# Who makes the remainders of the first mixer's output-projection weights: two chunks from VectorE to GpSimd

## The reference

```python
def hgrn2_mixer(h, w_in, lower_bound, g_norm_w, w_out):
    q, f, i, g = jnp.split(h @ w_in, 4, axis=-1)
    ...
    fg = lb + (1.0 - lb) * jax.nn.sigmoid(heads(f))
    o = hgrn2_chunkwise(jax.nn.silu(heads(q)), 1.0 - fg, heads(i), jnp.log(fg))
    o = o * lax.rsqrt(jnp.mean(jnp.square(o), -1, keepdims=True) + RMS_EPS)
    o = o * g_norm_w.astype(jnp.float32) * jax.nn.silu(heads(g))
    return o.reshape(B, S, D).astype(h.dtype) @ w_out
```

## Time and profile before

| | |
|---|---|
| median of three runs | 1483.66 us (1483.12 to 1487.24) |
| span of the profiled execution | 1483.1 us |
| busy: PE, DVE, ACT, POOL | 1452.5, 859.6, 615.7, 482.5 us |
| the last mixer iteration | about 225 to 255 us |

### The profile page before, as it was taken

The page is one execution under the profiler, slowest core; times in us unless marked ns, Lnnn a source line. Parts: engine busy times, 40 slices in busy tenths (PEclk is TensorE's granted clock), DMA queues, the critical chain, the costliest instruction groups (busy, mean ns, idle before and its releaser), DMA issues.

```text
span 1483.1 us, 23698 instructions
## 1 busy us (share of the span) xinstructions
PE 1452.5 (98%) x9390; PEld 1207.6 (81%) x9390; DVE 859.6 (58%) x1261; ACT 615.7 (42%) x780; POOL 482.5 (33%) x360
## 2 busy tenths in 40 slices
PE   8999999999999999999999999999999999999999
PEld 6787887898888888899777988888888897777677
DVE  7787686576665660165686666656630374565741
ACT  5565554353223221245574442232221355655541
POOL 0000000225544545432221145445454524422222
PEclk9999999999999999999999999999999999999999
DMA  7422122403222233323102122222323312322211
GB/s 222 136 74 87 58 86 102 156 29 114 85 92 106 87 112 113 112 87 106 66 30 86 57 86 85 95 103 88 110 85 112 129 58 86 130 74 71 72 56 59
DMA packets 23601, 137.25 MB, mean 93 GB/s; under 512 B 2600, under 2 KB 5208, under 8 KB 8672
## 3 DMA queue, kind: packets, MB, share of 16 engines
q1 hardware_dynamic: 18288, 124.79, 23.9%
q10 hardware_dynamic: 5232, 11.32, 2.8%
HBM read 131.89 MB, written 4.21 MB: 92 GB/s over the span
## 4 chain that ended last, share of the span: by engine, by line
issue 41%; PE 27%; POOL 24%; DVE 3%; DMA 2%; ACT 1%; DVEq 1%; POOLq 0%; ACTq 0%; SPq 0%
POOL WL L468 15%; POOL WL L477 9%; PE pair L503 7%; PE pair L505 6%; PE pair L504 6%; DMA RAW<-stream 1%; PE pair L1096 1%; PE pair L1083 1%; DVE WL L1672 1%; PE pair L688 1%; PE pair L1015 1%; PE pair L1073 1%; PE pair L717 1%; ACT WH L1202 1%; DMA PAR<-params 0%
## 5 line engine op out<-in xcount | busy, mean ns | idle before, releaser
L503 PE MATMUL pair<-AH,WH 128*128 128x512 f32 (+1 forms) x1240 | 473.4, 382 | 9.4 <-DVE AL L1661 6.6
L468 POOL TENSOR_TENSOR WL<-RAW,WH 128x512 fp32r<-128x512 f32 x228 | 310.5, 1394 | 475.6 <-ACT WH L1202 475.6
L505 PE MATMUL pair<-AH,WL 128*128 128x512 f32 (+1 forms) x1240 | 462.6, 373 | 0.0
L504 PE MATMUL pair<-AL,WH 128*128 128x512 f32 (+1 forms) x1240 | 462.4, 373 | 0.0
L1202 ACT ACTIVATE WH<-RAW 128x2048 fp32r<-128x2048 f32 x106 | 202.8, 1913 | 455.5 <-PE pair L505 446.4
L477 POOL TENSOR_TENSOR WL<-RAW,WH 128x512 fp32r<-128x512 f32 x128 | 171.8, 1374 | 506.8 <-ACT WH L1202 506.8
L503 PEld LDWEIGHTS pair<-AH,WH 128*128 128x128 f32 x1240 | 233.5, 188 | 58.5 <-issue 15.9
L505 PEld LDWEIGHTS pair<-AH,WL 128*128 128x128 f32 x1240 | 233.0, 188 | 41.8
L504 PEld LDWEIGHTS pair<-AL,WH 128*128 128x128 f32 x1240 | 233.5, 188 | 41.1 <-issue 1.9
L2042 DVE TENSOR_SCALAR CA<-pair,PAR 128x512 f32<-128x512 f32 x88 | 67.3, 806 | 147.4 <-PE pair L505 144.4
L503 PE MATMUL pair<-GH,WH 128*128 (+2 forms) x416 | 148.7, 357 | 0.1
(11 more groups left out here) (249 smaller groups left out, 1890.4 us busy)
## 6 DMA issues: line engine op xcount, KB each, us to landing
RAW<-stream SPq DMA_DIRECT2D x114, 1024.0 KB, 4.9
H<-x_t SPq DMA_DIRECT2D x5, 512.0 KB, 6.6
bias_rows<-ROWS ACTq DMA_DIRECT2D x1, 2048.0 KB, 24.5
BIAS<-bias_rows ACTq DMA_DIRECT2D x1, 2048.0 KB, 7.8
FBC<-forget_rows ACTq DMA_DIRECT2D x4, 512.0 KB, 4.0
out<-H ACTq DMA_DIRECT2D x8, 256.0 KB, 2.0
H<-x_t SPq DMA_DIRECT2D x1, 1024.0 KB, 10.4
RAW<-stream SPq DMA_DIRECT2D x3, 256.0 KB, 6.7
```

The lines of the kernel that those rows point to most:

```text
L468: pool.tensor_tensor(WL[w][:, part], RAW[raw][:, part], WH[w][:, part].bitcast(F32), ALU.subtract).then_inc(w_lo, 1)
L503: pe.matmul(out_, wh, xh, start=start, stop=False, skip_group_check=shared)
L504: pe.matmul(out_, wh, xl, start=False, stop=False, skip_group_check=shared)
L505: return pe.matmul(out_, wl, xh, start=False, stop=stop, skip_group_check=shared)
```

## The change

Chunks 16 and 17 leave `BY_DVE`: VectorE's two calls of `split_lo` in the last iteration go, and with them the row form in `split_lo`. GpSimd's first span starts two chunks earlier and covers four chunks. The counts follow: SP's loads of chunks 18 and 19 and TensorE's first uses of chunks 16 and 17 wait on `w_lo`, no longer on `hg_lo`.

```diff
-        BY_DVE = range(1, N_HO + 2)
+        BY_DVE = range(1, N_HO)
...
-            return 4 * (n + (-1 - N_HO - (extras_before(n) if skip is None else skip)))
+            return 4 * (n + (1 - N_HO - (extras_before(n) if skip is None else skip)))
...
-            span(split_rows, N_HO + 2, 2)
+            span(split_rows, N_HO, 4)
...
-                    if part % 2 == 0 or n >= N_HO:
+                    if part % 2 == 0:
...
-                    if n >= N_HO:
-                        raw, wh, wl = (a.rearrange("p (k c) -> p k c", k=2) for a in (raw, wh, wl))
...
-                        part = (slice(None), slice(None), slice(512 * half, 512 * half + 512)) if n >= N_HO else (slice(None), slice(1024 * half, 1024 * half + 1024))
+                        part = (slice(None), slice(1024 * half, 1024 * half + 1024))
...
-                split_lo(HG_F[it + 1] if not last else N_HO)
+                if not last:
+                    split_lo(HG_F[it + 1])
...
-                split_lo(HG_V[it + 1] if not last else N_HO + 1)
+                if not last:
+                    split_lo(HG_V[it + 1])
```

## The result

The changed kernel takes 1488.67 us (median of 15 runs, 1487.15 to 1490.13), the kernel before 1484.34 us in the same comparison (15 runs, 1483.06 to 1488.96). The recorded ratio is 1.0024 with an interval of 1.0017 to 1.0031 (the two medians by themselves are 4.3 us apart, a quotient of 1.0029). So the change costs 2.5 to 4.6 us, most likely 3.6. That is real, since the interval leaves out 1; it lies under the prediction's bound of 0.3% by the ratio, while the upper end of the interval lies just above it.

What follows compares the result with a forecast made beforehand. VectorE's chain into TensorE's hole ahead of level 5 was taken to bound the change. Terms 0 + 0 + 3.3 = +3.3 us on the median 1483.66 gave 1486.96, rounded 1487.0; range 1484.0 to 1488.8.

Steps and rivals of the forecast that it cites:

- rival (b): Ahead of level 5: all four GpSimd quarters precede line 1733, since ScalarE is not held up; +4.1 us, 1487.8, chance 0.18.
- the forecast of two or three quarters ahead: Second set, chunk 17: two or three GpSimd quarters precede line 1733; 1485.9 or 1487.0 us, chance 0.55.
- rival (c): Behind TensorE's hole ahead of level 5: the stretch at 1.2 GHz grows too; +5.0 us, 1488.7, chance 0.1.
- The bound and the path: VectorE from 237.2 to 244.9 us: any lengthening goes one to one into TensorE's hole ahead of level 5.
- Parts 1 and 2: Splits of chunks 16 and 17 leave VectorE: gain 0, for chunk 17 at most 0.1 us, as VectorE waits for TensorE.
- Part 3: GpSimd's quarters and VectorE's operations with two SBUF inputs take turns; one of each together lasts 1.7 us.
- Part 4: First set, chunk 16, from 225.7 us: turns make VectorE 0.85 us later, chunk 17's rounding ends at 242.9; path cost 0.
- Part 5: Second set, chunk 17, from about 243.0 us: turns start level 5 3.3 us later; 2.2 with two quarters ahead, bounds 0 and 4.1.
- the cover of level 3: TensorE wants `scale_qk(3, 3)` from about 237.05 us; delayed to about 236.4, it still holds by 0.6 us.
- Nothing swallows the delay: Behind level 5 TensorE's order is full and later waits, also at 274.39, hang on its own progress; nothing is given back.

Runs made afterwards that it cites:

- chunk 16 alone: GpSimd makes only chunk 16's remainder and chunk 17 goes back to VectorE, otherwise the changed kernel; ratio to the kernel before 1.0002 (0.9993 to 1.0012).
- the eighths: Changed kernel, but GpSimd makes chunk 17 in eight parts of 128x256, not four of 128x512; ratio to the kernel before 1.0015 (0.9996 excluded: 1.0006 to 1.0024).
- the late chunk 17: Changed kernel, but in the last iteration ScalarE rounds chunk 17 behind level 6's exponent; ratio to the kernel before 1.0005 (0.9996 to 1.0014).
- the fills: Changed kernel, but for chunk 17 GpSimd only writes zeros into WL and its remainder is left out; wait ahead of level 5 2.31 us, no time given.
- the three later starts: Changed kernel with GpSimd's first set later, by delayed rounding of chunk 16 or one or three fills; waits ahead of level 5 4.45, 4.46, 4.45 us.
- variants with one and with three fills: Changed kernel with one or three fills of zeros ahead of GpSimd's first quarter of chunk 16, which overwrites them; no time given.

## Why the prediction was right, and where it was not

The time lies 1.7 us above the forecast of 1487.0 and inside the range, 0.1 us under its upper end. Of the 1.7, 0.7 us is the kernel before, whose median is 1484.34 in the larger set of runs and not 1483.66; 0.7 is the wait, which grew by 4.03 and not by 3.3; 0.3 is left over, less than the executions of one kernel scatter (3 us and more). The ratio, 1.0024 against 1.0022 forecast, agrees better than the mechanism does, and that is luck: the term was too small, and about 1 us of what the hole cost was given back behind it, which the prediction had ruled out. What took place in the trace is rival (b), with a chance of 0.18, and not the forecast of two or three quarters ahead. That the measured 1488.7 is also the number of rival (c) is luck of the same kind.

- **The bound and the path** (VectorE's chain into TensorE's hole): right. The wait went from 2.31 to 6.34 and carried through to `outputs`.
- **Parts 1 and 2, nothing gained on VectorE**: right. `pick(3, 2)` still waited 1.72 us for TensorE, at 237.17; `pick(3, 6)` followed level 6 with no split ahead of it. Shown also by chunk 16 alone, 1.0002.
- **Part 3, the price of a turn**: right. An operation that waits for its turn takes 1.75 us, about 1.7 per turn as estimated; that it is exclusion by whole instructions is shown by the eighths, the late chunk 17 and the fills.
- **Part 4, the first set: this step failed.** It had turns from the start, `shift(3, 4)` 0.85 us late, and the rounding of chunk 17 ending at 242.9. Instead VectorE's four ran through at once, GpSimd's second quarter standing back for 2.6 us; turns came only with the next `shift`, and its end was no later than before. ScalarE's exponent started at 234.41, its rounding of chunk 17 at 240.08, and GpSimd's second set at 242.06. The prediction's reading that the exponent of level 4 starts 0.18 us behind `shift(3, 4)` is also not what set it: in both kernels it starts 0.71 us behind ScalarE's own copy of the turned keys, which it follows in ScalarE's list, with no wait for VectorE. The changed kernel, and the kernel before:

```profile
233.70 0.81 ACT L1303 ACTIVATE KD<-pair 128x768 f32<-128x768 f32 x1 [4.19 <-PE pair L696]
234.41 1.06 ACT L1287 ACTIVATE DD<-DD 128x1024 f32<-128x1024 f32 x1
...
240.08 1.90 ACT L1202 ACTIVATE WH<-RAW 128x2048 fp32r<-128x2048 f32 x1
...
233.77 0.81 ACT L1303 ACTIVATE KD<-pair 128x768 f32<-128x768 f32 x1 [1.92 <-PE pair L696]
```

- **Part 5, the term of 3.3 us**: mis-sized for that reason; all four quarters lay ahead of line 1731, rival (b), with 4.1 forecast and 4.03 measured as wait. That the dependence in part 4 is real is shown by the three later starts: where turns are taken, ScalarE is late and two quarters are ahead, 4.45 us of wait, 2.14 more than before, where part 5 gave 2.2 for that case. The same variants show that the cover of level 3 was thinner than part 4 had it: where all four operations took turns, level 3 waited 0.6 us.
- **Nothing swallows the delay**: wrong by about 1 us of 4. TensorE's wait for GpSimd at 274.39 gave back 0.35 us, and 0.7 more came back up to 771 us. In the kernel before, GpSimd's first quarter of chunk 18 took 1.69 us, because it met VectorE's last half of the extra chunks (later weights that VectorE splits, line 1868), which ended at 270.6. In the changed kernel that half began earlier, relative to the rest, and hardly met the quarter, which took 1.33 us. VectorE starts on the extra chunks without the 0.44 us of issue time that the kernel before has there; why is open. SP's loads of chunks 18 and 19 came 4.2 and 1.6 us later, not 1.5 and 1, and cost nothing: the roundings of both chunks waited for TensorE in both kernels.
- **Rival (c), the clock**: its mechanism came true and its cost did not, in this execution. The stretch at the low clock doubled, from 3.4 to 6.8 us, but half of it fell into the hole: before, TensorE worked 3.4 us at 0.51; in the changed kernel the clock was low for the second half of the hole (0.73 over 6.2 us) and then for 3.4 us of work at 0.50. Which part falls on work is not set by the hole alone. With the eighths, TensorE worked 4.8 us at the low clock. The variants with one and with three fills have the same hole, up to 247.77 us, and the first then works 5.7 us at the low clock, the second 3.3 us. In the other fourteen runs of the changed kernel, of which there is no trace, part of the stretch may have cost time. The kernel before, the eighths, then the variants with one fill and with three:

```profile
245.10:248.50 3.40, 3.40 (x70) 2.71 (x70) 3.23 (x8) 0.00 (x0) 0.00 (x0) 0.51 0.24 69
...
246.70:251.50 4.80, 4.76 (x136) 3.69 (x139) 2.55 (x6) 0.00 (x0) 3.45 (x4) 0.50 0.26 81
...
251.10:253.40 2.30, 2.30 (x130) 1.76 (x128) 0.88 (x4) 0.00 (x0) 0.00 (x0) 0.50 0.57 125
...
251.10:253.40 2.30, 2.30 (x133) 1.87 (x132) 1.43 (x7) 0.00 (x0) 0.00 (x0) 1.00 0.61 119
```

**Open.** Which of the two goes first when a quarter and VectorE's run ask at nearly the same time. The long quarter asked 0.4 us into the 0.68 us copy, and stood back for four operations; in two other runs it asked at the copy's start and stood back for the rest of it alone. It was 3.85 to 3.86 us long in all six kernels whose first set starts as in the changed one, so it is no scatter, but the cause isn't found. The 0.7 us given back between 278 and 771 us were not studied.

## What to carry to other kernels

Before handing element-wise work with SBUF inputs to an idle GpSimd, look at what VectorE does at that moment, not at its busy share: beside VectorE operations with two SBUF inputs each GpSimd instruction costs VectorE up to its own length. If the work must overlap, make its instructions short, or place it where the critical chain does not run or reads one operand from PSUM. The work taken from VectorE gained nothing here because both pieces lay in its waits for TensorE; the order of the chain into TensorE's hole was worth about 2.2 us, and who does the side work nothing (chunk 16) or a loss (chunk 17).

## What the runs showed of the hardware

- The exclusion has the grain of an instruction: 128x512 operations of VectorE went from 0.69 to 1.75 us beside parts of 128x512 on GpSimd, and to 1.21 beside parts of 128x256.
- Turn-taking is not guaranteed: one GpSimd instruction that takes 1.27 us otherwise lasted 3.86 us while four VectorE operations in a row kept their 0.68.
- Fills by GpSimd (0.53 us for 128x512) do not disturb VectorE's two-input operations. VectorE's copies within SBUF are held up by a reading GpSimd, 2.14 against 1.18 us for four.
- Holes in TensorE's work of 2.3 us were followed by 3.4 us of work at 1.2 GHz in four traces, at once or up to 1.3 us after work had begun again; one of 0.83 us by none. Equal holes did not cost the same: behind a wait of 4.45 us, work at 1.2 GHz lasted 3.3, 5.7 and 6.1 us in three traces, and behind one of 6.34 us only 3.4.
